# Two low parts of x made by ScalarE and an adding transfer, and one PSUM copy placed earlier, at the entry of a Trainium2 FFN

## The chip, the cores and the metric

The kernel runs on one NeuronCore of one Trainium2 chip. The metric is the device time of one execution in microseconds: 1799.57 us, the median of three runs (1797.29 to 1799.92). The engines are TensorE (PE; its weight loads are PEld), VectorE (DVE), ScalarE (ACT), GpSimd (POOL) and SyncE (SP). Each executes its own queue in order and waits at semaphores for the others.

## The reference

Three residual blocks on x of 512 tokens by 1024 channels in float32: a conformer convolution, a dilated attention, and a second block that begins and ends with a SwiGLU FFN of width 2816 around a mixer. The change is in the two FFNs alone:

```python
def swiglu_ffn(x, g, w_gate, w_up, w_down):
    h = rms_norm_2(x, g)
    return (jax.nn.silu(h @ w_gate) * (h @ w_up)) @ w_down
...
x = x + 0.5 * swiglu_ffn(x, ffn1_norm[l], ffn1_w_gate[l], ffn1_w_up[l], ffn1_w_down[l])
```

## The kernel before

**High and low parts.** A float32 operand is used as the sum of a high part (float32r, rounded) and a low part, the rest. A product takes three matmuls: high by high, high by low, low by high. ScalarE makes the high part by a copy. For weights it also writes the negated rounded copy into the place of the low part (L629), and GpSimd issues a transfer that adds the raw weight onto it (`low`, L550, `accum_op=ALU.add`), so the transfer does the subtraction. VectorE makes the low parts of activations by a subtraction (L1422, L1352).

**Weights.** 289 tiles of 128 x 1024 pass through a ring of four slots. SyncE loads slot n when the low part of tile n - 4 has landed (and, for joined tiles, when its sums are made). ScalarE prepares a tile when its raw data has landed and TensorE is through with the tile four before it.

**The FFN stages** are stages 7 and 13 (`ffn` on each engine, f = 0 and 1). The 22 column blocks m of the width 2816 are worked off in three spans of 8, 8 and 6, each followed by 8 tiles of the down product. Blocks 0 to 2 are plain: one gate tile and one up tile, each of 24 matmuls of 128 x 512 (L2103), read from PSUM by VectorE, silu on ScalarE, then mid = silu(gate) x up, split into mid_hi and mid_lo. Blocks 3 to 21 are joined: gate and up of one block against the two halves of the tokens form a 2 x 2 product of quarters, computed by seven products instead of eight. Each product is 12 matmuls of 128 x 256 (L2213). I number them 1 to 7 in the order of issue; they use the operands 0, 1, 3, 4, 5, 2 and 6 of x. Product 4 adds onto the PSUM region of product 1, so product 1 must first be copied out (into var, by `keep`); product 6 adds onto the region of product 3 (copied into r0, shown as r), product 7 onto that of product 4 (copied into rs).

**Operands of x** are the quarters of the normalised x and sums of them. `x_high` (ScalarE) makes their high part, `x_low` (VectorE) their low part. x_first and x_second hold the two halves of the channels. Operands 0, 1 and 2 are plain quarters, in B_hi and B_lo; 1 and 2 lie in x_second, as 4 pieces of 256 tokens (1 KB each) per partition. Operands 3 to 6 are differences or sums (`t_operand`, L1536 and L1538) which are written over the quarters: number 4 over quarter 2, number 5 over quarter 1. Their high and low parts take the place of H_hi and H_lo, which the plain tiles read.

**The order** on each engine is written out by hand. On VectorE, after the plain block 1: low parts of operands 1 and 2, multiply, mid_lo, the three sums of operands 4 to 6, the four sums of weights for block 3 (w_sum), the low parts s_lo, then the low parts of operands 3 to 6 mixed with block 2. On ScalarE: copies of B, weights, mid_hi, and from s_hi on the weight sums and the H_hi of operands 3 to 6; var of block 3 comes in `period(3)`. TensorE issues product 3 of block 3 when its s_lo and H_lo are there.

## Time and profile before

| | |
|---|---|
| median of 3 runs | 1799.57 us |
| the profiled execution | 1800.54 us, its span 1798.5 us |
| TensorE busy | 1764.0 us, 98% |
| VectorE busy | 1148.9 us, 64% |
| ScalarE busy | 1173.7 us, 65% |
| GpSimd busy | 315.2 us, 18% |
| DMA queue of GpSimd | 148.40 MB, 43.5% of 16 engines |
| DMA queue of SyncE | 156.00 MB, 27.5% of 16 engines |
| joined products, L2213 | six kinds of matmul of 128 x 256, x456 each |

The span runs from the first to the last record of the execution; its device time has 2 us more around it. Busy shares are means over stages with different limits. What a wait costs is read at the place where it stands, and an idle time counts only on the engine that bounds the stage.

### The profile page before, as it was taken

To read this page: it belongs to the slowest core of one execution; us is meant where nothing else is said; L and a number is where in the kernel's file an instruction comes from. 1 tells how busy PE (TensorE), PEld (TensorE's weight loads), DVE (VectorE), ACT (ScalarE), POOL (GpSimd) and SP (SyncE) were. 2 spreads that over 40 slices of the span, in tenths; PEclk is the share of its full clock that TensorE was granted. 3 is DMA by queue.
4 is the path that set the end of the run, shared out by engine and by line. 5 is a ranking of instruction groups with operands and counts; after the bars stand their busy time and mean duration, and the time that the engine had idled before them with its cause. 6 is when DMAs were issued, how large, how long until landed. Compare 5 with 4: busy or idle time off the path is not lost.

```text
span 1798.5 us, 26833 instructions
## 1 busy us (share of the span) xinstructions
PE 1764.0 (98%) x10357; PEld 1463.7 (81%) x10357; DVE 1148.9 (64%) x1962; ACT 1173.7 (65%) x1742; POOL 315.2 (18%) x409
## 2 busy tenths in 40 slices
PE   8999999999999998999999999999999989999999
PEld 6788678777787886989989876767777879899897
DVE  5999667756657678627537465696754477276372
ACT  6777768666666776646647675666675667466473
POOL 1222011332322111111111111001111111111111
PEclk9999999999999999999999999999999999999999
DMA  8899698766665686787887976445656867878877
GB/s 240 191 210 206 170 228 203 170 158 142 151 151 131 177 193 150 176 202 173 191 192 178 256 192 153 117 117 129 153 129 169 200 163 173 197 177 191 194 175 183
DMA packets 93647, 317.05 MB, mean 176 GB/s; under 512 B 12368, under 2 KB 12496, under 8 KB 92752
## 3 DMA queue, kind: packets, MB, share of 16 engines
q0 software_dynamic: 47440, 148.40, 43.5%
q1 hardware_dynamic: 43488, 156.00, 27.5%
q10 hardware_dynamic: 2592, 10.94, 1.7%
q8 instruction: 83, 1.36, 0.3%
q14 instruction: 44, 0.36, 0.1%
HBM read 160.88 MB, written 6.29 MB: 93 GB/s over the span
## 4 chain that ended last, share of the span: by engine, by line
PE 79%; DVE 13%; ACT 4%; issue 2%; DMA 1%; DVEq 0%; ACTq 0%
PE ps L2103 45%; PE ps L2213 21%; DVE cv_acc L1649 4%; PE ps L2120 3%; DVE tmp L1649 3%; PE ps L2178 2%; PE ps L2441 1%; PE ps L2453 1%; ACT w_hi L615 1%; DMA w_lo<-w_raw 1%; PE ps L2696 1%; PE ps L2657 1%; PE ps L2482 1%; PE ps L2741 1%; ACT w_lo L629 1%
## 5 line engine op out<-in xcount | busy, mean ns | idle before, releaser
L550 POOL DMA_DIRECT2D w_lo<-w_raw x289 | 249.8, 865 | 1363.7 <-ACT w_lo L629 1281.9
L615 ACT ACTIVATE w_hi<-w_raw 128x1024 fp32r<-128x1024 f32 (+1 forms) x289 | 288.0, 997 | 135.6 <-PE ps L2103 121.2
L2103 PE MATMUL ps<-H_hi,w_hi 128*128 128x512 f32 x648 | 265.1, 409 | 5.6 <-DMA w_lo<-w_raw 5.6
L629 ACT ACTIVATE w_lo<-w_raw 128x1024 fp32r<-128x1024 f32 x251 | 263.0, 1048 | 0.0
L2103 PE MATMUL ps<-H_lo,w_hi 128*128 128x512 f32 x648 | 252.5, 390 | 0.0
L2103 PE MATMUL ps<-H_hi,w_lo 128*128 128x512 f32 x648 | 252.5, 390 | 0.0
L1345 DVE SCALAR_TENSOR_TENSOR X<-ps,X 128x512 f32<-128x512 f32 (+1 forms) x68 | 49.2, 723 | 174.3 <-PE ps L2103 166.4
L2103 PEld LDWEIGHTS ps<-H_hi,w_hi 128*128 128x128 f32 x648 | 121.7, 188 | 39.7 <-issue 10.0
L2103 PEld LDWEIGHTS ps<-H_lo,w_hi 128*128 128x128 f32 x648 | 121.8, 188 | 30.4 <-issue 6.5
L2213 PE MATMUL ps<-H_hi,s_hi 128*128 128x256 f32 x456 | 130.9, 287 | 13.6 <-DVE H_lo L1422 7.4
L2103 PEld LDWEIGHTS ps<-H_hi,w_lo 128*128 128x128 f32 x648 | 121.6, 188 | 25.9
L2103 PE MATMUL ps<-mid_hi,w_hi 128*128 128x512 f32 x352 | 137.3, 390 | 1.5 <-DVE mid_lo L1352 1.5
L2103 PE MATMUL ps<-mid_lo,w_hi 128*128 128x512 f32 x352 | 137.0, 389 | 0.0
L2103 PE MATMUL ps<-mid_hi,w_lo 128*128 128x512 f32 x352 | 136.9, 389 | 0.0
L2213 PE MATMUL ps<-H_hi,s_lo 128*128 128x256 f32 x456 | 130.6, 286 | 0.0
L2213 PE MATMUL ps<-H_lo,s_hi 128*128 128x256 f32 x456 | 130.5, 286 | 0.0
L2213 PE MATMUL ps<-B_hi,w_hi 128*128 128x256 f32 x456 | 129.2, 283 | 0.0
L2213 PE MATMUL ps<-B_lo,w_hi 128*128 128x256 f32 x456 | 129.2, 283 | 0.0
L2213 PE MATMUL ps<-B_hi,w_lo 128*128 128x256 f32 x456 | 129.2, 283 | 0.0
L2103 PE MATMUL ps<-N_hi,w_hi 128*128 128x512 f32 x280 | 116.7, 417 | 0.0
L2103 PE MATMUL ps<-N_hi,w_lo 128*128 128x512 f32 x280 | 109.4, 391 | 0.0
L2103 PE MATMUL ps<-N_lo,w_hi 128*128 128x512 f32 x280 | 109.3, 390 | 0.0
(426 smaller groups left out, 4135.2 us busy)
## 6 DMA issues: line engine op xcount, KB each, us to landing
w_raw<-weights SPq DMA_DIRECT2D x289, 512.0 KB, 4.3
w_lo<-w_raw POOLq DMA_DIRECT2D x251, 512.0 KB, 5.3
w_lo<-w_raw POOLq DMA_DIRECT2D x38, 256.0 KB, 4.7
cv_yl<-cv_a POOLq DMA_DIRECT2D x8, 256.0 KB, 3.9
pl_P<-spill ACTq DMA_DIRECT2D x1, 2048.0 KB, 9.7
spill<-X ACTq DMA_DIRECT2D x8, 256.0 KB, 6.9
X<-spill ACTq DMA_DIRECT2D x2, 1024.0 KB, 6.0
out<-X SPq DMA_DIRECT2D x8, 256.0 KB, 4.3
```

The costliest lines, as they stand in the source:

```text
L550: pool.dma_start(w_lo[:, u, 0:width], w_raw[:, u, 0:width], accum_op=ALU.add).then_inc(lo_landed[u], 16)
L615: return act.activation(out_ap, in_ap, ACT.Copy)
L629: act.activation(w_lo[:, s, :].bitcast(F32R), w_raw[:, s, :], ACT.Copy, scale=-1.0).then_inc(hi_done, 1)
L1345: dve.scalar_tensor_tensor(X[:, m:m + n, :], src, scale, X[:, m:m + n, :], ALU.mult, ALU.add)\
L1649: dve.scalar_tensor_tensor(acc, a[:, 0:S - t], w, acc, ALU.mult, ALU.add).then_inc(dve_chain, 1)
L2103: mm = pe.matmul(ps[:, bank, :], w, x, start=first and n == 0 and q == 0, stop=last and n == len(blocks) - 1 and q == 2, skip_group_check= ...
L2120: mm = pe.matmul(ps[:, banks[which], :], w, x[:, b, :], start=b == 0 and q == 0, stop=b == KC - 1 and q == 2, skip_group_check=True)
L2178: pe.matmul(ps[:, bank, :], ones if lhsT is None else lhsT, sq[:, (k.n[sq_done] - 1) % 2, :], start=c == 0, stop=c == n - 1).then_inc(sq_u ...
L2213: mm = pe.matmul(region(m, of), a, x, start=begins and b == 0 and q == 0, stop=b == 3 and q == 2, skip_group_check=True)
L2441: mm = pe.matmul(ps[rows, 6, r * P + q0:r * P + q1], at_V[:, 3 * (a % 2) + g, v * P + rows.start:v * P + rows.stop], turned_home(a, u)[:, ...
L2453: mm = pe.transpose(ps[:, turned_bank(u), n * P:(n + 1) * P], probs[:, b * P:(b + 1) * P], ident)
L2482: mm = pe.matmul(ps[:, n, :], w, x[:, b, :], start=b == 0 and q == 0, stop=b == 3 and q == 2, skip_group_check=True)
```

## The change

ScalarE makes a second, negated copy of operands 1 and 2 into B_lo directly behind their high parts. GpSimd adds the raw operand onto each by a transfer, between the low parts of the fifth and the sixth tile of the stage. TensorE waits for these two transfers where it waited for VectorE, and VectorE waits for both of them ahead of the first sum that is written over x_second. VectorE's two subtractions go. The copy of product 1 of block 3 into var is taken out of `period(3)` and put behind the high parts of operands 3 and 4. The semaphore that counts the high parts now goes up by nine a stage and the one of the low parts by five.

```diff
--- before.py
+++ after.py
@@ -73,7 +73,7 @@
 QUARTER = D // 2
 HALF = S // 2
 REGIONS = (0, 2, 5, 4)
-X_STEPS, OPERANDS, PRODUCTS, OUTS, COPIES = 6, 7, 5, 4, 4
+X_STEPS, OPERANDS, HIGHS, PRODUCTS, OUTS, COPIES = 6, 5, 9, 5, 4, 4
 READS = (8, 8, 8, 8, 40, 4, 8, PLAIN + 24, 0, 28, 16, 4, 8, PLAIN + 24, 0)
 TILES = (26, 3, 8, 8, 40, 4, 8, len(FFN_TILES), 0, 28, 16, 4, 8, len(FFN_TILES), 0)
 TILES0 = [sum(TILES[:n]) for n in range(15)]
@@ -341,6 +341,7 @@
         x_ready = sem("x_ready")
         operand_hi = sem("operand_hi")
         operand_lo = sem("operand_lo")
+        x_low_landed = [sem(f"x_low_landed{i}") for i in range(2)]
         w_summed = sem("w_summed")
         sum_hi = sem("sum_hi")
         sum_lo = sem("sum_lo")
@@ -599,6 +600,12 @@
                     low(first + SLOTS * c + j)
             for n in range(first + 4 * SLOTS, sum(TILES)):
                 low(n)
+                for f, stage in enumerate(FFNS):
+                    if n == TILES0[stage] + 4:
+                        for i in (1, 2):
+                            pool.wait_ge(operand_hi, HIGHS * f + 2 * i + 1)
+                            pool.dma_start(operand(False, i).bitcast(F32), raw_operand(i), accum_op=ALU.add)\
+                                .then_inc(x_low_landed[i - 1], 16)
 
 
         @block.scalar
@@ -748,6 +755,8 @@
 
                     act.wait_ge(x_ready, X_STEPS * f + steps)
                     copy(operand(True, i), raw_operand(i)).then_inc(operand_hi, 1)
+                    if i in (1, 2):
+                        act.activation(operand(False, i), raw_operand(i), ACT.Copy, scale=-1.0).then_inc(operand_hi, 1)
 
                 def silu(m):
 
@@ -786,7 +795,8 @@
                 def period(m):
 
                     a, b = part_of(m)
-                    keep(m, var, 0, 1)
+                    if m > PLAIN:
+                        keep(m, var, 0, 1)
                     if m > a:
                         mid_high(m - 1)
                     keep(m, r0, 5, 3)
@@ -824,6 +834,7 @@
                 act.wait_ge(tile_done, base + 2 * PLAIN)
                 x_high(3, 3)
                 x_high(4, 4)
+                keep(PLAIN, var, 0, 1)
                 mid_high(2)
                 x_high(5, 5)
                 x_high(6, 6)
@@ -1418,7 +1429,7 @@
 
                 def x_low(i):
 
-                    dve.wait_ge(operand_hi, OPERANDS * f + i + 1)
+                    dve.wait_ge(operand_hi, HIGHS * f + i + 1 + 2 * (i > 2))
                     dve.tensor_tensor(operand(False, i), raw_operand(i), operand(True, i).bitcast(F32), ALU.subtract)\
                         .then_inc(operand_lo, 1)
 
@@ -1550,10 +1561,10 @@
                 t_operand(3, quarter(0, 1), quarter(0, 0), ALU.subtract, 3)
                 plain_gate(1)
                 plain_up(1)
-                x_low(1)
-                x_low(2)
                 multiply(1)
                 mid_low(1)
+                for landed_x in x_low_landed:
+                    dve.wait_ge(landed_x, 16 * (f + 1))
                 t_operand(4, quarter(1, 1), quarter(0, 1), None, 4)
                 t_operand(5, quarter(1, 1), quarter(1, 0), ALU.add, 5)
                 t_operand(6, quarter(1, 1), quarter(0, 0), ALU.subtract, 6)
@@ -2228,7 +2239,10 @@
                         return quarters(s_hi[:, m % 2, :], n), quarters(s_lo[:, m % 2, :], n)
 
                     def x_operand(i):
-                        pe.wait_ge(operand_lo, OPERANDS * f + i + 1)
+                        if i in (1, 2):
+                            pe.wait_ge(x_low_landed[i - 1], 16 * (f + 1))
+                        else:
+                            pe.wait_ge(operand_lo, OPERANDS * f + i + 1 - 2 * (i > 2))
 
                     def bank_read(n):
                         if m in (SPANS[1][0], SPANS[2][0]):
```

Line numbers after the change are 7 to 11 higher in the parts shown. In the rows below, w_raw, w_hi and w_lo are weight tiles, mid_hi and mid_lo the two parts of the FFN's middle product, sq and tmp the gate and the up part, s_hi the high parts of weight sums.

ScalarE, first FFN stage, behind the preparation of the fifth plain tile (x_second holds operands 1 and 2). Before:

```order
L629 ACTIVATE w_lo<-w_raw 128x1024
L615 ACTIVATE B_hi<-x_second 128x1024 [waits x_ready] x2
L615 ACTIVATE mid_hi<-tmp 128x512 [waits tmp_done]
L615 ACTIVATE w_hi<-w_raw 128x1024 [waits tile_done,landed2]
L629 ACTIVATE w_lo<-w_raw 128x1024
L754 ACTIVATE sq<-sq 128x512 [waits scaled]
L615 ACTIVATE w_hi<-w_raw 128x1024 [waits tile_done,landed3]
L629 ACTIVATE w_lo<-w_raw 128x1024
L615 ACTIVATE mid_hi<-tmp 128x512 [waits tmp_done]
```

After:

```order
L636 ACTIVATE w_lo<-w_raw 128x1024
L622 ACTIVATE B_hi<-x_second 128x1024 [waits x_ready]
L759 ACTIVATE B_lo<-x_second 128x1024
L622 ACTIVATE B_hi<-x_second 128x1024 [waits x_ready]
L759 ACTIVATE B_lo<-x_second 128x1024
L622 ACTIVATE mid_hi<-tmp 128x512 [waits tmp_done]
L622 ACTIVATE w_hi<-w_raw 128x1024 [waits tile_done,landed2]
L636 ACTIVATE w_lo<-w_raw 128x1024
L763 ACTIVATE sq<-sq 128x512 [waits scaled]
L622 ACTIVATE w_hi<-w_raw 128x1024 [waits tile_done,landed3]
L636 ACTIVATE w_lo<-w_raw 128x1024
L622 ACTIVATE mid_hi<-tmp 128x512 [waits tmp_done]
```

Each of the two B_hi copies is followed by a B_lo copy, and all that comes after stands two copies further back.

ScalarE, some 14 rows on, at the high parts of operands 3 to 6. Before:

```order
L615 ACTIVATE H_hi<-x_first 128x1024 [waits x_ready,tile_done]
L615 ACTIVATE H_hi<-x_second 128x1024 [waits x_ready]
L615 ACTIVATE mid_hi<-tmp 128x512 [waits tmp_done]
L615 ACTIVATE H_hi<-x_second 128x1024 [waits x_ready]
L615 ACTIVATE H_hi<-x_first 128x1024 [waits x_ready]
L615 ACTIVATE w_hi<-w_raw 128x512 [waits tile_done,landed2]
L731 ACTIVATE w_lo<-w_raw 128x512
L615 ACTIVATE var<-ps 128x256 [waits product_done]
L615 ACTIVATE r<-ps 128x256 [waits product_done]
L615 ACTIVATE s_hi<-w_sum 128x1536 [waits w_summed]
L615 ACTIVATE rs<-ps 128x256 [waits product_done]
```

After:

```order
L622 ACTIVATE H_hi<-x_first 128x1024 [waits x_ready,tile_done]
L622 ACTIVATE H_hi<-x_second 128x1024 [waits x_ready]
L622 ACTIVATE var<-ps 128x256 [waits product_done]
L622 ACTIVATE mid_hi<-tmp 128x512 [waits tmp_done]
L622 ACTIVATE H_hi<-x_second 128x1024 [waits x_ready]
L622 ACTIVATE H_hi<-x_first 128x1024 [waits x_ready]
L622 ACTIVATE w_hi<-w_raw 128x512 [waits tile_done,landed2]
L738 ACTIVATE w_lo<-w_raw 128x512
L622 ACTIVATE r<-ps 128x256 [waits product_done]
L622 ACTIVATE s_hi<-w_sum 128x1536 [waits w_summed]
L622 ACTIVATE rs<-ps 128x256 [waits product_done]
```

The var copy stands ahead of mid_hi instead of behind the weight quarter; the r, s_hi and rs copies keep their order.

VectorE, first FFN stage, plain block 1 and the sums of x. Before:

```order
L1435 TENSOR_TENSOR sq<-ps,rx 128x512 [waits tile_done,x_ready]
L1441 TENSOR_TENSOR tmp<-ps,rx 128x512 [waits tile_done]
L1422 TENSOR_TENSOR B_lo<-x_second,B_hi 128x1024 [waits operand_hi,read_out]
L1422 TENSOR_TENSOR B_lo<-x_second,B_hi 128x1024 [waits operand_hi]
L1447 TENSOR_TENSOR tmp<-sq,tmp 128x512 [waits gated]
L1352 TENSOR_TENSOR mid_lo<-tmp,mid_hi 128x512 [waits split_hi,tmp_done]
L1536 SCALAR_TENSOR_TENSOR x_second<-x_second,x_first 128x4x256
L1538 TENSOR_TENSOR x_second<-x_second 128x4x256 [waits x_ready]
L1538 TENSOR_TENSOR x_first<-x_second,x_first 128x4x256 [waits x_ready]
```

After:

```order
L1446 TENSOR_TENSOR sq<-ps,rx 128x512 [waits tile_done,x_ready]
L1452 TENSOR_TENSOR tmp<-ps,rx 128x512 [waits tile_done]
L1458 TENSOR_TENSOR tmp<-sq,tmp 128x512 [waits gated,read_out]
L1363 TENSOR_TENSOR mid_lo<-tmp,mid_hi 128x512 [waits split_hi,tmp_done]
L1547 SCALAR_TENSOR_TENSOR x_second<-x_second,x_first 128x4x256 [waits x_low_landed1,x_low_landed0]
L1549 TENSOR_TENSOR x_second<-x_second 128x4x256 [waits x_ready]
L1549 TENSOR_TENSOR x_first<-x_second,x_first 128x4x256 [waits x_ready]
```

The two B_lo rows are gone, and the first sum over x_second (L1536, now L1547) waits for two landings. On GpSimd two rows `B_lo<-x_second` stand between the 18th and the 19th of the 20 low parts of whole weight tiles that lead up to block 3, each waiting for operand_hi.

## Rows read from the trace of the kernel before

**Rows 1.** The page, its part 1: busy us (share of the span) and instructions.
```profile
PE 1764.0 (98%) x10357; PEld 1463.7 (81%) x10357; DVE 1148.9 (64%) x1962; ACT 1173.7 (65%) x1742; POOL 315.2 (18%) x409
```

**Rows 2.** The line of the joined products, L2213: TensorE idle before it, by releaser.
```profile
  ACT var L615: 13.0, 4
  DVE H_lo L1422: 7.4, 2
```

**Rows 3.** TensorE in time at both FFN entries: start, us, engine, line, what, [idle<-releaser].
```profile
713.71 0.36 PE L2213 MATMUL ps<-H_hi,s_hi 128*128 128x256 f32 x1 [3.96 <-DVE H_lo L1422]
...
719.22 0.58 PE L2213 MATMUL ps<-H_hi,s_hi 128*128 128x256 f32 x1 [3.61 <-ACT var L615]
...
721.94 0.41 PE L2213 MATMUL ps<-H_hi,w_hi 128*128 128x256 f32 x1
...
727.68 0.28 PE L2213 MATMUL ps<-B_hi,w_hi 128*128 128x256 f32 x1
...
1485.59 0.39 PE L2213 MATMUL ps<-H_hi,s_hi 128*128 128x256 f32 x1 [2.61 <-ACT var L615]
...
1491.49 0.28 PE L2213 MATMUL ps<-H_hi,s_hi 128*128 128x256 f32 x1
...
1492.93 0.28 PE L2213 MATMUL ps<-B_hi,w_hi 128*128 128x256 f32 x1
```

**Rows 4.** TensorE's waits from 1500 to the end: total us, times, longest.
```profile
PE ps L2103 <- DVE mid_lo L1352: 0.7, 1, 0.7
```

**Rows 5.** VectorE in time, first FFN stage.
```profile
696.09 2.36 DVE L1422 TENSOR_TENSOR B_lo<-x_second,B_hi 128x1024 fp32r<-128x1024 f32 x2
...
700.43 1.22 DVE L1536 SCALAR_TENSOR_TENSOR x_second<-x_second,x_first 128x1024 f32<-128x1024 f32 x1
...
712.34 1.23 DVE L1422 TENSOR_TENSOR H_lo<-x_first,H_hi 128x1024 fp32r<-128x1024 f32 x1 [0.99 <-ACT H_hi L615]
...
716.94 1.23 DVE L1422 TENSOR_TENSOR H_lo<-x_second,H_hi 128x1024 fp32r<-128x1024 f32 x1 [0.19 <-ACT H_hi L615]
```

**Rows 6.** ScalarE in time, first FFN stage; the last row is of the second.
```profile
689.60 2.01 ACT L615 ACTIVATE B_hi<-x_second 128x1024 fp32r<-128x1024 f32 x2 [0.61 <-DVE x_second L1428]
...
694.75 0.63 ACT L754 ACTIVATE sq<-sq 128x512 f32<-128x512 f32 x1 [0.72 <-DVE sq L1435]
...
699.08 0.63 ACT L615 ACTIVATE mid_hi<-tmp 128x512 fp32r<-128x512 f32 x1 [1.80 <-DVE tmp L1447]
...
718.80 0.36 ACT L615 ACTIVATE var<-ps 128x256 f32<-128x256 f32 x1
...
723.26 0.37 ACT L615 ACTIVATE rs<-ps 128x256 f32<-128x256 f32 x1
...
1489.64 0.37 ACT L615 ACTIVATE rs<-ps 128x256 f32<-128x256 f32 x1
```

**Rows 7.** The page, its part 5: negated copies, busy us, mean ns.
```profile
L629 ACT ACTIVATE w_lo<-w_raw 128x1024 fp32r<-128x1024 f32 x251 | 263.0, 1048 | 0.0
```

**Rows 8.** GpSimd in time: the issue of the fifth plain tile's low part.
```profile
689.28 0.86 POOL L550 DMA_DIRECT2D w_lo<-w_raw  x1 [4.42 <-ACT w_lo L629]
```

**Rows 9.** DMA by window (689-690, 694-696, 684-689, 720.5-722.5, 689-695): landing us, queue share.
```profile
w_lo<-w_raw POOLq DMA_DIRECT2D x1, 512.0 KB, 5.0
...
w_lo<-w_raw POOLq DMA_DIRECT2D x1, 512.0 KB, 6.7
...
q0 software_dynamic: 144, 0.52, 53.0%
...
w_lo<-w_raw POOLq DMA_DIRECT2D x1, 512.0 KB, 4.4
...
q0 software_dynamic: 144, 0.26, 72.3%
...
q1 hardware_dynamic: 144, 0.52, 25.3%
```

**Rows 10.** One stretch: us, busy us of the engines, PEclk, DMA share, GB/s.
```profile
720.00:724.00 4.00, 4.00 (x21) 4.00 (x20) 2.75 (x5) 2.13 (x3) 0.06 (x1) 0.50 0.59 111
```


## The prediction

> **What bounds the kernel now.** I read the page's busy shares first: TensorE is busy for 98% of the span [rows 1], so time is won only where it stands still or runs at the lower clock. The view of one line, the matmul line of the joined products (L2213), then gives its idle time by releaser: 13.0 us in 4 waits for ScalarE's copy into var, 7.4 us in 2 waits for VectorE's H_lo [rows 2]. The timeline of TensorE puts the long ones at the entry of each of the two FFN stages. In the first FFN stage product 3 of block 3 starts at 713.71 after 3.96 us of waiting for H_lo, product 4 at 719.22 after 3.61 us of waiting for var, and block 4 begins at 727.68; in the second stage product 4 waits 2.61 us and block 4 begins at 1492.93 [rows 3]. Behind that there is next to nothing: from 1500 to the end TensorE waits once, 0.7 us [rows 4]. What block 4 gains at its start should therefore reach the end of the kernel, and what it loses too.
>
> The order before product 3 comes from the chain of waits and the timelines of VectorE and ScalarE. Product 3 needs H_lo of operand 3 (VectorE, 712.34 + 1.23 = 713.57). That is the end of one closed line of work which starts with the differences of x at 700.43 (L1536) and goes through the four weight sums, s_hi on ScalarE and s_lo [rows 5]. What delays the 700.43 delays product 3, and with it the later H_lo of operand 5 (716.94 + 1.23 = 718.17) [rows 5] and ScalarE's rs copy (723.26 + 0.37 = 723.63) [rows 6], for which products 5 and 7 wait.
>
> **First part: the var copy goes ahead.** Before, var is copied at 718.80, behind mid_hi, two H_hi and a weight quarter [rows 6]. Afterwards it stands directly behind the H_hi of operands 3 and 4, which end near 713.2 (ScalarE then idles until the multiply behind the H_lo of operands 3 and 4 has run, near 715.3, so the copy's 0.36 us cost nothing there). A product is 12 matmuls and takes 1492.93 - 1491.49 = 1.44 us at full clock, 2.53 us at half (719.22 to about 721.75, just ahead of the row at 721.94) [rows 3]. Without any delay in the line above, in the first stage: product 3 at 713.71, product 4 at 715.15, product 5 at 718.2 (H_lo of operand 5), product 6 at 719.7, product 7 at 723.7, because it now waits for the rs copy, and block 4 at 725.1. Against 727.68 that is 2.6 us. So of the 3.6 us wait taken away not all comes back: H_lo of operand 5 and the rs copy are late next. Second stage: the rs copy ends at 1489.64 + 0.37 = 1490.01 [rows 6], block 4 starts at 1490.05 + 1.44 = 1491.5 against 1492.93, 1.4 us. Sum of this part: -4.0 us. The rest of the copy's successors on ScalarE (r, s_hi, rs) start at most 0.3 us earlier.
>
> **Second part: VectorE gives up two low parts.** It frees 2.36 us at 696.09 [rows 5]. I value this at zero. ScalarE gets the two negated copies in exchange. Two copies in a row took 2.01 us [rows 6], a negated one alone 1.05 [rows 7], so each further one adds 0.96 us, 1.9 us in all. From 691.5 on everything on ScalarE is 1.9 us later, the weight low part for the sixth plain tile included. The silu at 694.75 waits for VectorE [rows 6], which waits for ScalarE's mid_hi before it, so it moves along, to 696.7. Ahead of the next mid_hi, at 699.08, ScalarE has 1.80 us of idle time [rows 6]; with the shift its queue reaches this copy at 699.1, the old time. The copy's input, the multiply after the silu, is now ready near 698.0, but the queue isn't. VectorE's mid_lo and the 700.43 therefore stay where they were, at best: VectorE idles in place of working.
>
> **The added wait.** L1536 now waits until both transfers have landed, since it overwrites x_second. Behind it on VectorE stands the whole closed line. The transfers go through GpSimd's queue between the low part of the fifth plain tile (issued at 689.28 [rows 8], landed 5.0 us later, 694.3 [rows 9]) and that of the sixth. Their issues can go out at about 691.9 and 693.8, when ScalarE's copies are done, so they queue directly behind the 694.3. What does such a transfer cost on the 16 DMA engines? One of 512 KB in rows of 4 KB took 53.0% of 5 us, 2.65 us; one of 256 KB in rows of 2 KB took 72.3% of 2 us, 1.45 us [rows 9]. Both have 128 rows, so bytes cost 1.20 us per 256 KB and 128 rows cost 0.25 us. Operands 1 and 2 are quarters of x in pieces of 1 KB, 512 of them: 2.40 + 1.00 = 3.4 us each. In between comes the load of a weight tile, which is issued when the 694.3 lands, 25.3% of 6 us, 1.5 us [rows 9]. Landing of the second: 694.3 + 3.4 + 3.4 + 1.5 = 702.6. L1536 starts 2.2 us later than 700.43. The trace has no accumulating transfer in pieces of 1 KB, so this is bounded from both sides: 2.65 us each, as for whole rows (701.1, delay 0.7), and 5.8 us each, if every piece costs as much as one of 2 KB, 4 x 1.45 (707.4, delay 7.0). I take 3.4 us, which is nearest to the two rows and fits both. Twice (the second stage has the same order with the same durations): +4.4 us.
>
> The Trainium skill gives another price: DMA: Bandwidth & Descriptors, "Anatomy of one DMA — SWDGE (gpsimd) path", fits a GpSimd transfer as 2.0 us and its bytes over 436 GB/s. By that, an estimate from the page, 512 KB take 3.2 us, the second would land near 697.0 and the delay would be nothing. The trace disagrees here: the accumulating transfers took 5.0 and 6.7 us to landing [rows 9].
>
> **What the transfers push back.** GpSimd's wait for the copies ends before the sixth tile's low part is ready, so nothing is held in the program's order, only on the DMA engines. It was issued after 694.3 and took 6.7 us [rows 9], to 701.1, about when TensorE came to it. Now it lands 2.65 us behind the 702.6, at 705.3: TensorE stands over 4 us at the sixth plain tile. Its 24 matmuls (5.5 us) end at 710.8, products 1 and 2 (2.9 us) at 713.7, with 1.7 us more if the clock falls in the pause. Product 3 would start at 713.71 + 2.2 = 715.9, so this wait lies in time that TensorE waits anyway. If that cover were gone it would cost all it exceeds it by. The reload of the ring slot follows later by the same 4 us, lands near 710 and is first read just ahead of the old place of the var copy, 718.80: hidden.
>
> **The clock.** In the first stage the granted clock was 0.50 from 720 to 724 [rows 10], which is the level of 1.2 GHz, after the two pauses of 3.96 and 3.61 us [rows 3]. The changed entry still has pauses of 1 to 4.5 us at other places. A product at 1.2 GHz costs 1.1 us more [rows 3], and that counts where it falls in product 7 or block 4, and is covered ahead of product 7. Between 0 and 1.7 us a stage, half a microsecond taken for each: +1.0 us.
>
> **Sum.** -4.0 + 4.4 + 1.0 = +1.4 us. On the profiled execution's 1800.54 us this gives 1801.9; that execution stood 1.0 us above the median of 1799.57, so I predict a median of 1801.0 us. I treat 0.2%, 3.6 us, as the least that a measurement of this kernel tells from no change.
>
> **Rivals.**
> Faster, because the transfers hide. If the second lands by 700.4, only the first part is left: -4.0 us, 1795.6. For it: an undisturbed low part landed 4.4 us after its issue [rows 9], and 693.8 + 4.4 = 698.2 would do. Against it: at just this place the sixth tile's low part took 6.7 us [rows 9] beside a weight load, and now two more stand in the same queue. It needs less than 2.3 us a transfer. The skill's fit named above would give this result, and by it the chance would be far higher; the 6.7 us hold it down. 0.10.
>
> Faster, because VectorE is what holds the line and 2.3 us a stage come off it as well: -4.0 - 4.6, 1791. That needs ScalarE's mid_hi to move up with it, and its queue is full up to 699.1. It is also the case in which nothing of my exchange holds. 0.03.
>
> Slower, because the pieces are dear. One mechanism: L1536 waits for B_lo, all of VectorE's line stands behind it. With the dear end of 5.8 us a transfer the delay is 7.0 us a stage: +14.0 - 4.0 = +10, 1809.6. Halfway, 4.6 us a transfer: landing 705.0, delay 4.6, -4.0 + 9.2 + 1.0 = +6.2, 1805.8, which I take as this case's time. It is slower than the limit from a delay of 3.3 us on, a transfer of 3.95 us. For it: no row shows a piece of 1 KB, and GpSimd's issue may grow with the count of pieces. Against it: the two rows lie on one straight line with a small share per row. 0.28.
>
> No change that can be told, with the delay eating the gain: 0.59, its own range 1797 to 1803.2.
>
> **How the numbers follow.** Faster by over 0.2%: 0.10 + 0.03 = 0.13; within: 0.59; slower: 0.28. The range goes from 1796.5 (delay 0.7 in both stages with no loss of clock gives -2.6, with the spread of the runs a little below) to 1807 (beyond the half-dear case), and leaves out some 0.07 below and 0.08 above.
>
> **What would show it.** Right: VectorE idle for some 2 us between mid_lo and the first difference on x_second, with a B_lo transfer as releaser; TensorE waiting 4 to 5 us for w_lo at the sixth plain tile; no wait for var at product 4 of block 3, instead waits for H_lo at product 5 and for rs at product 7; mid_hi on ScalarE at the same time as before. Wrong: B_lo landing under 5 us after its issue; mid_hi at 697; product 3 released by its own tile's weights or by the plain tile and not by H_lo; a block 4 in which TensorE waits again, which would mean that the gain is not carried to the end.

## The result and the profile after

| kernel | median (lowest to highest), runs | profiled execution | its span |
|---|---|---|---|
| before | 1799.57 us (1797.29 to 1799.92), 5 | 1800.54 us | 1798.5 us |
| after | 1804.89 us (1803.75 to 1808.15), 5 | 1803.75 us | 1801.7 us |

The ratio is 1.0037, with a 95% interval from 1.0025 to 1.0050: the change makes the kernel slower by 0.25 to 0.5% (the ratio is taken over all runs; the two medians alone give 1.0030). The time lies inside the range of the prediction, 3.9 us above its value, and nearer to the slow rival's 1805.8 than to the forecast.

The timeline of VectorE after the change, first FFN stage; it answers to [rows 5]. Columns: start in us, duration in us, engine, line, operation and tiles, number of instructions, and in brackets the idle time before it and what ended it.

```profile
697.21 0.69 DVE L1363 TENSOR_TENSOR mid_lo<-tmp,mid_hi 128x512 fp32r<-128x512 f32 x1 [1.73 <-ACT mid_hi L622]
700.84 1.22 DVE L1547 SCALAR_TENSOR_TENSOR x_second<-x_second,x_first 128x1024 f32<-128x1024 f32 x1 [2.95 <-DMA B_lo<-x_second]
...
712.75 1.23 DVE L1433 TENSOR_TENSOR H_lo<-x_first,H_hi 128x1024 fp32r<-128x1024 f32 x1 [0.90 <-ACT H_hi L622]
...
717.36 1.23 DVE L1433 TENSOR_TENSOR H_lo<-x_second,H_hi 128x1024 fp32r<-128x1024 f32 x1 [0.18 <-ACT H_hi L622]
```

VectorE finishes mid_lo at 697.9 and then stands for 2.95 us, released by a B_lo transfer. Times of two executions can't be compared as they stand, since each reaches the stage at a time of its own. So all that follows is counted from ScalarE's first B_hi copy of x_second, which comes before every moved instruction: 689.60 in the kernel before [rows 6], 687.01 after. The first difference on x_second then starts at +10.83 before (700.43) and at +13.83 after.

ScalarE's timeline after, the same stretch, for [rows 6]:

```profile
687.01 1.06 ACT L622 ACTIVATE B_hi<-x_second 128x1024 fp32r<-128x1024 f32 x1 [0.62 <-DVE x_second L1439]
687.98 1.04 ACT L759 ACTIVATE B_lo<-x_second 128x1024 fp32r<-128x1024 f32 x1
...
694.06 0.63 ACT L763 ACTIVATE sq<-sq 128x512 f32<-128x512 f32 x1 [0.72 <-DVE sq L1446]
...
696.49 0.61 ACT L622 ACTIVATE mid_hi<-tmp 128x512 fp32r<-128x512 f32 x1
...
713.50 0.36 ACT L622 ACTIVATE var<-ps 128x256 f32<-128x256 f32 x1
...
723.68 0.36 ACT L622 ACTIVATE rs<-ps 128x256 f32<-128x256 f32 x1
```

The mid_hi copy starts at +9.48, exactly as before (699.08 - 689.60), but without the 1.80 us of idle time: the two negated copies have filled it. The var copy is early and free, and stands 10 us before rs.

The timeline of TensorE after, both entries, for [rows 3]:

```profile
703.28 0.80 PE L2114 MATMUL ps<-H_hi,w_hi 128*128 128x512 f32 x1 [5.11 <-DMA w_lo<-w_raw]
...
714.12 0.36 PE L2224 MATMUL ps<-H_hi,s_hi 128*128 128x256 f32 x1
...
718.64 0.39 PE L2224 MATMUL ps<-H_hi,w_hi 128*128 128x256 f32 x1 [1.41 <-DVE H_lo L1433]
...
724.09 0.38 PE L2224 MATMUL ps<-H_hi,s_hi 128*128 128x256 f32 x1 [2.33 <-ACT rs L622]
...
726.22 0.41 PE L2224 MATMUL ps<-B_hi,w_hi 128*128 128x256 f32 x1
...
737.20 0.28 PE L2224 MATMUL ps<-B_hi,w_hi 128*128 128x256 f32 x1
...
1493.13 0.58 PE L2224 MATMUL ps<-H_hi,s_hi 128*128 128x256 f32 x1 [2.32 <-ACT rs L622]
...
1495.86 0.42 PE L2224 MATMUL ps<-B_hi,w_hi 128*128 128x256 f32 x1
...
1506.11 0.28 PE L2224 MATMUL ps<-B_hi,w_hi 128*128 128x256 f32 x1
```

No product waits for var. Product 5 (718.64) waits for H_lo and product 7 (724.09) for rs. The rows at 737.20 and 1506.11 are the first of block 5, where both entries are over. The same point in the kernel before, and the start of its second entry on ScalarE:

```profile
737.76 0.28 PE L2213 MATMUL ps<-B_hi,w_hi 128*128 128x256 f32 x1
...
1503.01 0.28 PE L2213 MATMUL ps<-B_hi,w_hi 128*128 128x256 f32 x1
```
```profile
1455.94 1.06 ACT L615 ACTIVATE B_hi<-x_second 128x1024 fp32r<-128x1024 f32 x1 [0.61 <-DVE x_second L1428]
```

Each entry, from the B_hi copy to block 5, took 48.16 and 47.07 us before. After, it took 50.19 and 49.86 us (the second begins at 1456.25). That is +4.8 us, against the 5.3 us between the two medians. The rest of the two executions differs by -2.6 us ahead of the first entry, +0.9 us between the entries and +0.1 us behind the second, in the range of what the kernels of this study show there, where no edit touches them (687.0 to 692.6 us ahead of the first entry, 718.1 to 719.9 us between the two). All together it is the +3.2 us of the spans. Counting by the length of the entries keeps this out, but it is still the length in one execution of each kernel.

The page of the kernel after, part 1, for [rows 1]; its matmul line of the joined products, idle time by releaser, for [rows 2]; and TensorE's waits from 1500 to the end, for [rows 4].

```profile
PE 1763.0 (98%) x10357; PEld 1462.8 (81%) x10357; DVE 1144.1 (64%) x1958; ACT 1175.7 (65%) x1746; POOL 315.3 (18%) x413
```
```profile
  ACT rs L622: 9.7, 4
  DVE H_lo L1433: 6.7, 5
```
```profile
PE ps L2114 <- DVE mid_lo L1363: 0.7, 1, 0.7
```

The idle time of the joined products fell from 20.4 us to 16.4 and the kernel became slower: idle time was exchanged for the wait at the sixth plain tile and for matmuls at half rate. Behind the entries nothing waits, so what they lose reaches the end.

Two windows of the kernel after, behind product 7 of both stages, for [rows 10]. Columns: stretch, length, busy us of PE, weight load, VectorE, ScalarE and GpSimd, granted clock, DMA share, GB/s.

```profile
725.00:728.00 3.00, 3.00 (x16) 3.00 (x16) 2.97 (x7) 3.00 (x5) 0.84 (x1) 0.50 0.51 206
1494.00:1496.00 2.00, 2.00 (x11) 2.00 (x11) 1.53 (x3) 2.00 (x3) 0.00 (x0) 0.50 0.79 320
```

TensorE is busy all the time, at 1.2 GHz, in product 7 and block 4, where nothing covers it.

GpSimd's timeline after, for [rows 8], then the DMA answers for the windows of the issues at 686.69, 689.31 and 691.21 (last number: us to landing), for [rows 9]:

```profile
686.69 0.84 POOL L551 DMA_DIRECT2D w_lo<-w_raw  x1 [4.43 <-ACT w_lo L636]
689.31 1.29 POOL L607 DMA_DIRECT2D B_lo<-x_second  x1 [1.78 <-ACT B_lo L759]
691.21 1.26 POOL L607 DMA_DIRECT2D B_lo<-x_second  x1 [0.61 <-ACT B_lo L759]
```
```profile
w_lo<-w_raw POOLq DMA_DIRECT2D x1, 512.0 KB, 5.5
...
B_lo<-x_second POOLq DMA_DIRECT2D x1, 512.0 KB, 5.7
...
B_lo<-x_second POOLq DMA_DIRECT2D x1, 512.0 KB, 9.5
```

The fifth tile's low part lands at 692.2, the first B_lo at 695.0 and the second at 700.7: 2.8 and 5.7 us apart. The load of a weight tile, issued when the fifth tile's low part has landed, ends at 699.3, in the second gap.

### The profile page after: what moved, and what is told of

The parts are those of the page before. It is cut to its first block, busy times and chain, and to the rows that moved or that the text cites. A ratio compares the mean times of both kernels' runs of the same rounds, so it can differ in the third digit from the quotient of the medians.

```text
span 1801.7 us, 26839 instructions
## 1 busy us (share of the span) xinstructions
PE 1763.0 (98%) x10357; PEld 1462.8 (81%) x10357; DVE 1144.1 (64%) x1958; ACT 1175.7 (65%) x1746; POOL 315.3 (18%) x413
## 4 chain that ended last, share of the span: by engine, by line
PE 75%; DVE 13%; ACT 5%; DMA 4%; issue 2%; ACTq 0%; DVEq 0%
PE ps L2114 42%; PE ps L2224 20%; PE ps L2131 3%; DVE tmp L1660 3%; DVE cv_acc L1660 3%; DMA w_lo<-w_raw 2%; PE ps L2189 2%; DMA B_lo<-x_second 1%; ACT w_hi L622 1%; PE ps L2455 1%; ACT w_lo L636 1%; PE ps L2467 1%; DMA w_raw<-weights 1%; PE ps L2710 1%; PE ps L2671 1%
## 5 line engine op out<-in xcount | busy, mean ns | idle before, releaser
L551 POOL DMA_DIRECT2D w_lo<-w_raw x289 | 245.3, 849 | 1360.9 <-ACT w_lo L636 1282.7
```

Of the source, the lines that this page charges most:

```text
L551: pool.dma_start(w_lo[:, u, 0:width], w_raw[:, u, 0:width], accum_op=ALU.add).then_inc(lo_landed[u], 16)
```

## The experiments

All entries in one table. "Line" is the start of the first difference on x_second behind the B_hi copy, "entry" the time from that copy to block 5; two numbers are the two stages. "Half rate" says in which stages the clock was 0.50 behind product 7, up to block 5. Each ratio is to the kernel before, run alongside on the same chip.

| kernel | ratio [95%] | median us | line | entry | both entries | half rate |
|---|---|---|---|---|---|---|
| before | 1 | 1799.57 | 10.83 / 10.87 | 48.16 / 47.07 | 0 | none |
| after | 1.0037 [1.0025, 1.0050] | 1804.89 | 13.83 / 13.63 | 50.19 / 49.86 | +4.8 | both |
| e1 var move alone | 0.9989 [0.9980, 0.9998] | 1798.14 | 10.84 / 10.87 | 45.70 / 45.72 | -3.8 | none |
| e2 transfers alone | 1.0036 [1.0023, 1.0048] | 1807.40 | 13.60 / 13.89 | 49.92 / 49.96 | +4.7 | none |
| e3 transfers left out | 0.9994 [0.9985, 1.0003] | 1799.96 | 10.81 / 10.80 | 47.16 / 45.66 | -2.4 | first |
| e4 e1, pause filled | 0.9983 [0.9974, 0.9992] | 1796.39 | 10.84 / 10.86 | 45.70 / 45.73 | -3.8 | none |
| e5 after, pause filled | 1.0014 [1.0005, 1.0022] | 1802.70 | 13.10 / 13.90 | 47.97 / 48.77 | +1.5 | none |
| e6 whole rows | 1.0006 [0.9996, 1.0015] | 1801.17 | 11.84 / 12.81 | 48.20 / 49.14 | +2.1 | both |
| e7 load held back | 0.9982 [0.9973, 0.9991] | 1796.97 | 10.80 / 10.80 | 47.15 / 47.15 | -0.9 | both |
| e8 one transfer | 0.9985 [0.9976, 0.9994] | 1796.81 | 9.90 / 9.90 | 44.76 / 45.38 | -5.1 | none |
| e9 e4, multiply first | 0.9967 [0.9954, 0.9979] | 1795.41 | 10.11 / 10.12 | 44.97 / 44.99 | -5.3 | none |
| e10 e7, pause filled | 0.9988 [0.9979, 0.9996] | 1798.42 | 10.81 / 11.86 | 45.67 / 46.72 | -2.8 | none |
| e11 e8, load held, filled | 0.9961 [0.9948, 0.9973] | 1794.24 | 9.90 / 9.90 | 44.75 / 44.76 | -5.7 | none |
| e12 before, load held | 0.9995 [0.9986, 1.0004] | 1799.38 | 10.84 / 10.86 | 48.25 / 46.85 | -0.1 | none |

One formula gives the entries of all kernels with the early var copy: 45.7 us, plus what the line starts later (or earlier) than +10.84, plus 1.45 us if the clock is at half rate behind product 7. For the kernel after, 45.7 + 2.99 + 1.45 = 50.14 (measured 50.19) and 45.7 + 2.79 + 1.45 = 49.94 (49.86); for e6, 48.15 and 49.12 (48.20, 49.14). One of 22 entries departs by more than 0.1 us, the second of e8 with 45.38 against 44.76. Its constants come from the kernels up to e8; for e9 to e11 the expectations below give 45.0, 45.7 and 44.8 us, which came but for the second stage of e10, where the line was late.

The entries are those of one execution, the ratio is that of many. For three kernels the two differ by more than the interval of the ratio: e1 (entries -3.8 us, interval -3.6 to -0.4), e8 (-5.1 us, interval -4.3 to -1.1) and e7 (-0.9 us, interval -4.9 to -1.6). So the entries show where time is won and lost, and the ratio what it is worth.

### e1: the var copy alone

```
+ keep(PLAIN, var, 0, 1)      # behind x_high(3, 3), x_high(4, 4)
- keep(m, var, 0, 1)          # for m == PLAIN
```

> The kernel before with the var copy moved alone, no transfers. Theory A (the move is worth 2.6 and 1.4 us in the two stages, but the pause it leaves ahead of product 7 lowers TensorE's clock behind it for some 3.4 us, 1.7 us a stage): 1795.6 to 1799.5 us, near 1799 if the clock falls in both stages; in the trace product 7 of block 3 waits for rs some 2.5 us and runs at 1.2 GHz. Theory B (the loss after the change came from the stand at the sixth plain tile and its clock, and the move itself gives its full 4.0 us): 1795.6 us, with product 7 at full clock. VectorE's first difference on x_second stays 10.8 us behind the first copy of x_second.

The entries are 2.46 and 1.35 us shorter, 3.8 us against the 4.0 of the prediction; the measured gain is some 2 us (0.4 to 3.6). TensorE's timeline in the second entry:

```profile
1482.36 0.39 PE L2215 MATMUL ps<-H_hi,w_hi 128*128 128x256 f32 x1 [1.41 <-DVE H_lo L1424]
...
1487.82 0.39 PE L2215 MATMUL ps<-H_hi,s_hi 128*128 128x256 f32 x1 [2.33 <-ACT rs L615]
```

The two waits foretold, and no more. The profiled execution kept its clock behind the second one; e3 below shows that this is not so in every execution, which would make the median gain smaller than this profile's. The times bear this out: of the eleven executions of e1 the six with a mean granted clock of 0.996 or more took 1793.97 to 1798.14 us, the five below it 1799.26 to 1800.49 us. The mean doesn't tell in which stretch the clock was lost.

### e2: the transfers alone

```
- keep(PLAIN, var, 0, 1)      # behind x_high(4, 4); var is copied in its old place
```

> The change with the var copy left in its old place. Theory A (VectorE's line starts 2.9 us late for the landings and everything behind it shifts): 5.8 us above the kernel before, 1805.4 us, no matter what TensorE does at the sixth plain tile. Theory B (the stand of 5 us at the sixth plain tile is what costs): its part not hidden ahead of product 3, under 1 us a stage, so 1800 to 1801.5 us. Theory C (ScalarE's two more copies cost): 1803.4 us, and the next mid_hi on ScalarE late.

It is as slow as the whole change (1.0036 against 1.0037, each within 0.13%; entries +4.7 against +4.8 us), so beside the transfers the var move is worth nothing that shows. TensorE's timeline and a window of it:

```profile
721.80 0.58 PE L2222 MATMUL ps<-H_hi,s_hi 128*128 128x256 f32 x1 [3.77 <-ACT var L622]
...
727.55 0.28 PE L2222 MATMUL ps<-H_hi,s_hi 128*128 128x256 f32 x1
```
```profile
723.00:727.00 4.00, 4.00 (x29) 4.00 (x28) 2.74 (x5) 2.54 (x5) 0.00 (x0) 0.77 0.68 166
```

Products 4 to 6 take 727.55 - 721.80 = 5.75 us, against 3 x 1.44 = 4.32 at full clock. Had they run at full clock, product 7 could have started at 726.1; rs was ready at 726.2 (its copy starts at 725.85 and takes 0.36). So the 3.77 us wait for var costs nothing by itself. What costs is the lower clock behind it, 1.4 us. In the kernel after that loss is gone, and one of the same size stands behind the wait for rs.

### e3: the transfers left out, the rest as in after

```
- pool.dma_start(operand(False, i), raw_operand(i), accum_op=ALU.add)
- dve.wait_ge(landed_x, 16 * (f + 1))       # and TensorE waits for ScalarE's copies
```

> The change without the two adding transfers and without the waits for them; the low parts of operands 1 and 2 stay the negated rounded copies, so this part of the computation is left out. ScalarE's two extra copies and the moved var copy stay. Theory A (the exchange between VectorE and ScalarE is free and worth nothing, only the landings cost): the same as the var copy moved alone, within 1 us. Theory C (ScalarE's copies cost 1.9 us a stage): 3.8 us above it. Theory D (VectorE's freed 2.4 us move its line ahead): below it by up to 4.7 us.

The line starts at +10.81 although VectorE has 2.36 us less to do and ScalarE 1.9 us more. That is the prediction's step on VectorE's freed time, worth zero. Product 7 waits 2.32 us for rs in both stages; the clock fell behind the first and not behind the second, and the first entry is 1.50 us longer (47.16 against 45.66). Among its eleven executions the five with a mean granted clock of 0.996 or more took 1795.72 to 1798.62 us, the six at 0.994 took 1799.96 to 1801.45 us.

### e4 and e5: the pause ahead of product 7 filled

```
+ if m == PLAIN:
+     pe.wait_ge(read_out, READ0[stage] + PLAIN)
+     for _ in range(8):
+         pe.matmul(ps[:, 3, 0:P], ones, ones)      # ahead of the wait for rs
```

> The var copy moved alone, and 8 extra matmuls of 128 x 128 in an unused bank ahead of product 7 of block 3, in time that TensorE would wait for rs. They add 1.7 us of work inside a pause of about 2.5 us. Theory A (the pause lowers the clock): the clock stays at 2.4 GHz behind it, up to 1.7 us a stage less than the var copy moved alone, 1795.6 to 1796.5 us. Theory B (no loss of clock there): no difference, or up to 0.5 us a stage more.

> The change with 8 extra matmuls of 128 x 128 ahead of product 7 of block 3, inside its wait for rs. Theory A (1.45 us a stage of the loss is the lower clock behind that wait, 2.9 us a stage the landings): 2 to 3 us below the change, 0.15 to 0.2% above the kernel before; block 5 starts 48.6 us behind the first copy of x_second in place of 50.2 and 49.9. Rival (the clock falls at the sixth plain tile's stand and stays an effect of that stand): no difference.

TensorE's timeline in e4 and the same window as in the kernel after. Each of the eight float32 matmuls stands there as two instructions, so the row says x16:

```profile
721.88 1.95 PE L2267 MATMUL ps<-con 128*128 128x128 f32 x16
724.31 0.38 PE L2215 MATMUL ps<-H_hi,s_hi 128*128 128x256 f32 x1 [0.47 <-ACT rs L615]
```
```profile
725.00:728.00 3.00, 3.00 (x27) 3.00 (x26) 2.97 (x6) 3.00 (x6) 0.77 (x1) 1.00 0.59 240
```

The fill moves nothing else. e4's entries are those of e1, whose clock had not fallen. In the measured time e4 lies 0.06% under e1, with intervals that overlap, so for this pair alone a gain is not shown; nine of its eleven executions had a mean granted clock of 0.996 or more, against six of e1's. In e5 the entries are 45.7 plus the delay of the line, 2.27 and 3.03, and the kernel after is faster by 0.2% with it: 1.0014 against 1.0037, intervals apart. Over all kernels with an early var copy the clock fell behind product 7 in 7 of 12 entries without the fill and in none of 10 with it.

### e6: whole rows in place of pieces

```
- pool.dma_start(operand(False, i), raw_operand(i), accum_op=ALU.add)
+ pool.dma_start(B_lo[:, i, :].bitcast(F32).rearrange("p (a s) -> p a s", a=2),
+                x_second[:, 2 * i - 2:2 * i, :], accum_op=ALU.add)
```

> The change, with the two adding transfers moving the same bytes of x_second in whole rows of 4 KB in place of pieces of 1 KB (so the low parts of operands 1 and 2 are left wrong; the reads of x_second stay guarded by the same waits). Theory A1 (the pieces cost: 3.4 us by my pricing against 2.65 us for whole rows): VectorE's first difference on x_second starts 1.5 us earlier behind the first copy of x_second than the 13.8 and 13.6 us of the change, so 12.2 us, and the time falls by some 3 us. Theory A2 (the DMA engines are taken by the weight load and by waiting, pieces matter little): under 0.5 us earlier, time within 1 us of the change.

The bytes are as many, but they are no longer those of the two operands. GpSimd's timeline in the first stage, and the DMA answers for the two issues; the last two rows are those of the second stage (issues at 1457.48 and 1459.37):

```profile
691.13 0.86 POOL L607 DMA_DIRECT2D B_lo<-x_second  x1 [1.78 <-ACT B_lo L759]
693.02 0.85 POOL L607 DMA_DIRECT2D B_lo<-x_second  x1 [1.03 <-ACT B_lo L759]
```
```profile
B_lo<-x_second POOLq DMA_DIRECT2D x1, 512.0 KB, 5.2
...
B_lo<-x_second POOLq DMA_DIRECT2D x1, 512.0 KB, 7.5
...
B_lo<-x_second POOLq DMA_DIRECT2D x1, 512.0 KB, 5.1
...
B_lo<-x_second POOLq DMA_DIRECT2D x1, 512.0 KB, 8.5
```

In the first stage the landings are at 696.3 and 700.5, 4.2 us apart in place of 5.7; in the second they are at 1462.6 and 1467.9, 5.3 us apart in place of 5.5. The delay of the line falls to 1.0 and 2.0 us, from 3.0 and 2.8. The fifth tile's low part landed 2.5 and 2.7 us ahead of the first transfer. The issue falls from 1.29 to 0.86 us, the value of other transfers of 128 rows [rows 8].

### e7: the weight load held behind the transfers

```
+ if n == TILES0[stage] + 8:
+     sp.wait_ge(x_low_landed[1], 16 * (f + 1))
```

> The change, with SyncE's load of the stage's ninth weight tile held back until the second low part has landed. Theory A1 (the load takes 1.5 us of the engines' time between the two transfers): VectorE's first difference on x_second starts about 1.5 us earlier, 12.2 us behind the first copy of x_second, the time falls by some 3 us. Theory A2 (the load's share is hidden by its latency, transfers alone fill the time): under 0.5 us earlier. The tile itself is first needed 20 us later and nothing waits for it in either case.

VectorE's timeline, and the DMA answers for the issues at 691.05 and 692.95:

```profile
699.55 1.22 DVE L1550 SCALAR_TENSOR_TENSOR x_second<-x_second,x_first 128x1024 f32<-128x1024 f32 x1
```
```profile
B_lo<-x_second POOLq DMA_DIRECT2D x1, 512.0 KB, 5.3
...
B_lo<-x_second POOLq DMA_DIRECT2D x1, 512.0 KB, 6.2
```

The fifth tile's low part landed at 693.7, the two transfers at 696.4 and 699.2, 2.7 and 2.8 us apart, and VectorE goes on at 699.55 without idle time. One load, moved by a few microseconds, takes away all of the delay (+10.80). So the transfers in pieces take 2.7 to 2.8 us each when they are alone, and the load between them costs 5.7 - 2.8 = 2.9 us, twice what was expected here. Beside the whole rows of e6 the same difference is 4.2 - 2.5 = 1.7 us in one stage and 5.3 - 2.7 = 2.6 us in the other. The TensorE wait at the sixth plain tile falls to 1.71 us. The entries still hold the half-rate stretch, 1.45 us each. Measured, it is 1.6 to 4.9 us below the kernel before, and the entries tell only 0.9. Part of the difference is the execution that was profiled: with 1798.74 us it is the second slowest of ten and stands 1.8 us above their median, at a mean granted clock of 0.996, where four others had 0.998 and took 1793.8 to 1796.1 us. Whether these kept the clock behind product 7 no profile shows, and it stays open.

### e8: one transfer, the other low part on VectorE

```
- for i in (1, 2):        + for i in (1,):          # GpSimd's transfers, ScalarE's copies
+ x_low(2)                                          # VectorE, ahead of multiply(1)
```

> The change with operand 1 alone by a transfer; operand 2 goes back to VectorE. Theory A (what costs is the landing of the second transfer, the first landed 2.9 us before VectorE's old time): VectorE's line starts where it did before the change, 10.8 us behind the first copy of x_second, and the time is that of the var copy moved alone, 0.1% below the kernel before. Rival (every transfer ahead of the sixth tile's low part costs through TensorE's stand there, 3.4 us longer per transfer): half of the change's loss, 0.15 to 0.2% above the kernel before.

VectorE's timeline, first stage:

```profile
695.45 1.23 DVE L1433 TENSOR_TENSOR B_lo<-x_second,B_hi 128x1024 fp32r<-128x1024 f32 x1
...
698.04 0.69 DVE L1363 TENSOR_TENSOR mid_lo<-tmp,mid_hi 128x512 fp32r<-128x512 f32 x1 [0.77 <-ACT mid_hi L622]
698.65 1.22 DVE L1547 SCALAR_TENSOR_TENSOR x_second<-x_second,x_first 128x1024 f32<-128x1024 f32 x1
```

The line starts at 698.65 - 688.75 = +9.90, 0.93 us earlier than before. With one more copy instead of two, ScalarE has room left, and with one low part less the multiply is earlier: both sides of the exchange have to move. In the second stage the entry is 0.62 us longer than the formula says: the sixth tile's low part landed 13.8 us behind the B_hi copy (12.1 in the first stage), TensorE waited 2.67 us for w_lo at the sixth plain tile, and VectorE then waited for TensorE's plain tile, which delayed the H_lo behind it.

```profile
1474.41 0.69 DVE L1452 TENSOR_TENSOR tmp<-ps,rx 128x512 f32<-128x512 f32 x1 [1.05 <-PE ps L2115]
```

### e9: no transfer, the multiply ahead of the low parts

```
+ multiply(1)
  x_low(1)
  x_low(2)
- multiply(1)
```

> The var copy moved and the pause filled, no transfers, and on VectorE the multiply of block 1 placed ahead of the low parts of operands 1 and 2 instead of behind them. Theory A (VectorE's line hangs on the multiply, ScalarE's mid_hi and mid_lo, not on VectorE's amount of work): the two low parts fill the wait for mid_hi, the line starts 0.7 us earlier a stage (10.1 us behind the first copy of x_second), block 5 at 45.0; 1.4 us below the filled kernel, 0.25% below the kernel before. Rival: VectorE's work decides, then no order of it helps and the line stays at 10.8 us.

ScalarE's timeline:

```profile
694.99 1.05 ACT L629 ACTIVATE w_lo<-w_raw 128x1024 fp32r<-128x1024 f32 x1
695.93 0.62 ACT L615 ACTIVATE mid_hi<-tmp 128x512 fp32r<-128x512 f32 x1
```

The mid_hi copy starts at +7.58 in place of +9.48, straight behind the weight copy: the 1.80 us of idle time were VectorE's two low parts. The line starts 0.73 us earlier, now held by the low parts themselves, and both entries are 0.7 us under 45.7.

### e10, e11 and e12: the load held back, combined

e10 is e7 with the fill, e11 is e8 with the load held behind its one transfer and with the fill. e12 is the control, the kernel before with that load held until the sixth plain tile's low part has landed:

```
+ if n == TILES0[stage] + 8:
+     sp.wait_ge(lo_landed[(n - 3) % RING], 16 * ((n - 3) // RING + 1))
```

> The change with the ninth tile's load held back until the second low part has landed, and the pause ahead of product 7 filled. Theory A (landings and clock are the whole of the loss): the line starts at 10.8 us, block 5 at 45.7 us in both stages, the time of the kernel with the var copy moved and the pause filled, 0.2% below the kernel before. Rival (something of the transfers costs outside the entry): block 5 at 45.7 us but the time above that kernel by over 0.1%.

> Operand 1 alone by a transfer, load held back until it has landed, pause filled. Theory A: the line starts at 9.9 us as with one transfer, block 5 at 44.8 us in both stages, 5.7 us of the entry's 95.2 us gained in all, 0.25 to 0.3% below the kernel before and the fastest of all. Rival (the median of one transfer is all there is): no better than one transfer alone, 0.15% below.

> The kernel before with the same load held back until the sixth plain tile's low part has landed. Theory A (the load costs only where VectorE waits for a landing): the sixth low part lands sooner than 6.7 us after its issue, TensorE's 0.3 and 0.9 us waits for it go, and the time stays within 0.1% of the kernel before, since product 3 waits for VectorE. Rival (the load in that place slows the stage in itself): 0.2% or more below the kernel before.

In e12 the DMA answer for the sixth plain tile's low part is the same in both stages:

```profile
w_lo<-w_raw POOLq DMA_DIRECT2D x1, 512.0 KB, 4.4
```

Before, with the load beside it, it took 6.7 us [rows 9] and, in the second stage, 7.3. So the load costs a transfer in whole rows 2.3 and 2.9 us, as much as it costs the one in pieces. TensorE's waits at this tile (0.3 and 0.9 us) go, as expected, but it then waits 1.0 and 1.8 us for the next low part, ahead of product 1. The control gives nothing (0.9995), so holding the load helps only where transfers need its place. In e10 the fill shows no gain over e7 in the measured time (0.9988 against 0.9982), though its profile has no half-rate stretch behind product 7; in its second stage the line was 1.0 us late again, released by a B_lo landing. The load was held there too; the second transfer landed 3.9 us behind the first, in place of 2.7. In this gap (1462 to 1464) the DMA rows have a packet that the first stage doesn't have, one of the instruction queue:

```profile
q8 instruction: 1, 0.02, 3.5%
```

3.5% of 16 engines in 2 us are 1.1 us of one engine, the size of the delay. No run tests whether it is the cause. With nearly all of the transfers' delay gone the change is no better than the var move alone (e4, 0.9983). e11 has entries of 44.75 and 44.76 us and is the fastest, 0.39% below the kernel before; e9, without any transfer, comes to 0.33% with an interval that overlaps.

## Why the prediction came out as it did

The range held and so did the steps on order and releasers, but the sum was 1.4 us where the entries show 4.8 and the medians 5.3. The outcome is the prediction's slower case, which it gave 0.28, and not the change within 0.2% to which it gave 0.59. By its own steps:

- **The var copy, -4.0.** e1 shows -3.8, and next late are H_lo of operand 5 and rs, as foretold. The reason given was incomplete. Product 7 needs rs, and in the kernel before rs is ready at 34.03 us behind the B_hi copy (723.63 - 689.60), so a wait at product 4 can't lengthen the entry while TensorE runs at full clock. The 2.6 and 1.4 us were matmuls at half rate behind the wait (the 0.50 of [rows 10]). Hence they aren't a term that adds to the others: e2 shows it worth nothing beside the transfers.
- **VectorE's freed 2.36 us, 0.** Right: mid_hi at the same +9.48 (after), the line at +10.81 with the transfers left out (e3). The rival in which VectorE holds the line needed an earlier mid_hi. Where ScalarE or the order allows that (+7.58 in e9, +8.56 in e8), the line does move up, but by 0.7 and 0.9 us, not by 2.3.
- **The added wait, +4.4.** Right in mechanism, too small in size: the delays are 3.0 and 2.8 us, +5.8. This is one of the two mis-sized terms. The landing was forecast at 13.0 us behind the B_hi copy (702.6 - 689.6) and came at 13.7 (700.7 - 687.0). The fifth tile's low part landed 0.5 us later than priced. The two gaps sum to 8.5 us against 8.3, but for other reasons than assumed: 2.8 us a transfer instead of 3.4, and 2.9 us for the load instead of 1.5. That the landing came out within 0.7 us is in part luck: one price too high, the other too low. The 1.5 us are the time of the load's own packets; what it takes from a transfer of the other queue stood in the same rows, 6.7 us to landing beside a load and 4.4 undisturbed [rows 9], a difference of 2.3, and e12 confirms it. VectorE then starts 0.1 us behind the landing.
- **The clock, +1.0.** This is the other mis-sized term, and the larger: 1.45 us in each stage, +2.9. The prediction had the price (1.1 us a product) and the place (product 7 and block 4) and then took half a microsecond between 0 and 1.7. In the changed order the last pause stands directly ahead of the part that nothing covers, so the loss is either nothing or all of it, and in the profiled execution it was all of it in both stages.
- **The wait at the sixth plain tile, hidden.** Right: 5.11 us for w_lo, and product 3 still starts at 714.12, just behind H_lo (712.75 + 1.23 = 713.98). The cover was used up in the first stage, where TensorE shows no idle time ahead of product 3 and H_lo and product 2 end together; in the second stage product 3 waited 0.67 us for H_lo. Of the signs of being wrong, a product 3 that H_lo doesn't release, this was a near miss.

With the measured sizes the sum is -3.8 + 5.8 + 2.9 = +4.9 us, and the entries show +4.8. Of the rivals, the faster one with hidden transfers was wrong for this kernel, but by the load alone: e7 is that case, and its entries gain. The Trainium skill's price for a GpSimd transfer, named there (DMA: Bandwidth & Descriptors, "Anatomy of one DMA — SWDGE (gpsimd) path"), gives 3.2 us from issue to end as an estimate; the traces disagree, with 5.3 and 6.2 us even when no load lies between (e7), each queued behind the transfer before it, and 4.4 us for the undisturbed low part [rows 9]. That both transfers of e7 land in time comes from their early issue, not from this price. The slow rival had pieces of 4.6 us, and there are none: its delay of 4.6 us didn't come, but a delay of 2.9 with two half-rate stretches costs nearly the same.

The chances put 0.59 on a time within 0.2%. The limit from which the prediction counted as slower was a delay of 3.3 us, at a fixed 0.5 us for the clock. With 1.45 us in its place it is about 2.4 us, which the measured delay exceeds.

## What to carry to other kernels

Where several waits stand in a row in front of one late releaser, taking one away gains only what the clock lost behind it, and the next pause can lose it again; ask which pause comes last before the uncovered work, and put small matmuls there if it can't be closed. A transfer that replaces an engine's instruction has to be priced with what lies in the queues beside it: here one load in between decided alone whether it was hidden. The price of such a neighbour is the difference between two landings, with it and without it, and not the time of its own packets. An exchange between two engines moves the line only if both sides come early: half of it (one transfer, one subtraction), or another order of the same instructions, gained what the whole of it lost.

## What the runs showed of the hardware

- GpSimd was busy for 1.29 us with the issue of 512 KB in pieces of 1 KB, and 0.86 us with the same bytes in whole rows (e6).
- A load of 512 KB on the hardware queue put back an accumulating transfer of 512 KB on the software queue by 2.9 us when it was in pieces of 1 KB (after against e7), and by 1.7 and 2.6 us (e6) or 2.3 and 2.9 us (before against e12) when it was in whole rows. Its own packets take 1.5 us of the 16 engines [rows 9].
- Without a load between them, accumulating transfers of 512 KB landed 2.7 to 2.8 us apart in pieces of 1 KB (e7); whole rows landed 2.5 and 2.7 us behind the transfer before them (e6).
- Behind the pause ahead of product 7 (1.7 us in one entry, 2.3 in most) the granted clock fell to 0.50 in 7 of 12 entries and stayed in the others, in one case in one stage and not in the other of the same execution (e3). Eight small matmuls in the pause left 0.5 us of it idle, and it fell in none of 10.
